# Weighted sums with the values as weights, two heads on the array's column halves, and the narrow projections of sparse attention packed into one tile

## What is computed

```python
# sparse attention: 8 heads, ONE key head and ONE value head of width 64, 4 index heads
xr, yr, q, k, v, iq, ik, iw = jnp.split(x @ w_in, ...)      # widths 512 512 512 64 64 256 64 4
dots = jnp.einsum("bthd,bsd->bths", iqb, ik)
isc = jnp.einsum("bths,bth->bts", jax.nn.relu(dots), iwb)   # then the best 128 of the causal keys
probs = jax.nn.softmax(logits, axis=-1)                     # logits with a slope per head
return jnp.einsum("bthk,btkd->bthd", probs, vsel)
# latent attention: 16 heads, keys of width 96, values of width 64, causal
probs = jax.nn.softmax(logits, axis=-1)
return jnp.einsum("bhts,bshd->bthd", probs, v)
```

## Time and profile before

| | |
|---|---|
| median of 3 runs | 2769.94 us (2769.45 to 2771.9) |
| the profiled execution | 2770.24 us, its span 2768.4 us |
| granted clock of TensorE, mean | 0.991 |
| PE busy | 2692.2 us, 97% of the span, 13514 records |
| DVE busy | 1228.7 us, 44% |
| ACT busy | 934.1 us, 34% |
| POOL busy | 921.5 us, 33% |
| sparse attention, first score to last turn-out | 1535.6 to 1602.6 us |
| latent attention, same | 2142.6 to 2295.0 us |

### The profile page before, as it was taken

How to read it: one execution, slowest core, us unless ns; L and a number is a source line. 1 busy time by engine, 2 the same in 40 slices (tenths; PEclk the granted TensorE clock), 3 DMA queues, 4 the chain that set the end, 5 groups by cost and what they waited for, 6 DMA issues and landing times.

```text
span 2768.4 us, 34791 instructions
## 1 busy us (share of the span) xinstructions
PE 2692.2 (97%) x13514; PEld 2214.7 (80%) x13514; DVE 1228.7 (44%) x1981; ACT 934.1 (34%) x1304; POOL 921.5 (33%) x221
## 2 busy tenths in 40 slices
PE   8999999999999999999999999999998999999998
PEld 7898787887788877888877788888876778888886
DVE  6566543353522234101269743704543564370453
ACT  3353422223433343222254534212234543421222
POOL 2321243444223213444432123444432112344441
PEclk9999999999999999999999999999999999999999
DMA  7531343543222212232221022222221112222221
GB/s 307 185 135 62 120 152 144 190 170 103 87 69 69 74 56 76 80 116 92 78 98 61 31 69 92 91 100 97 92 84 50 43 47 69 92 91 99 98 91 61
DMA packets 44170, 271.37 MB, mean 98 GB/s; under 512 B 5087, under 2 KB 8695, under 8 KB 15896
## 3 DMA queue, kind: packets, MB, share of 16 engines
q1 hardware_dynamic: 40032, 266.23, 27.4%
q10 hardware_dynamic: 4024, 3.54, 0.6%
HBM read 267.62 MB, written 2.13 MB: 97 GB/s over the span
## 4 chain that ended last, share of the span: by engine, by line
PE 69%; issue 22%; POOL 5%; DVE 3%; ACT 1%; POOLq 0%; DVEq 0%; ACTq 0%
PE lin L711 20%; PE lin L713 19%; PE lin L712 19%; POOL wlo L676 5%; PE lin L1243 2%; PE bank L1263 2%; PE bank L1255 1%; PE lin L853 1%; PE bank L1548 0%; PE bank L870 0%; PE bank L1419 0%; DVE tmp L3015 0%; PE bank L1399 0%; PE bank L1230 0%; ACT whi L1720 0%
## 5 line engine op out<-in xcount | busy, mean ns | idle before, releaser
L676 POOL TENSOR_TENSOR wlo<-raw,whi 128x2048 fp32r<-128x2048 f32 (+3 forms) x213 | 921.0, 4324 | 1809.7 <-ACT whi L1720 1809.7
L711 PE MATMUL lin<-hhi,whi 128*128 128x512 f32 x1976 | 782.6, 396 | 10.9 <-DVE hlo L2492 2.5
L713 PE MATMUL lin<-hhi,wlo 128*128 128x512 f32 x1976 | 770.7, 390 | 0.0
L712 PE MATMUL lin<-hlo,whi 128*128 128x512 f32 x1976 | 770.2, 390 | 0.0
L1720 ACT ACTIVATE whi<-raw 128x2048 fp32r<-128x2048 f32 (+3 forms) x213 | 384.3, 1804 | 949.8 <-PE lin L713 886.0
L711 PEld LDWEIGHTS lin<-hhi,whi 128*128 128x128 f32 x1976 | 371.6, 188 | 99.7 <-issue 11.8
L711 PE MATMUL lin<-ghi,whi 128*128 128x512 f32 x1120 | 438.8, 392 | 4.4 <-POOL wlo L676 2.4
L713 PE MATMUL lin<-ghi,wlo 128*128 128x512 f32 x1120 | 436.7, 390 | 0.0
L712 PE MATMUL lin<-glo,whi 128*128 128x512 f32 x1120 | 436.4, 390 | 0.0
L713 PEld LDWEIGHTS lin<-hhi,wlo 128*128 128x128 f32 x1976 | 371.3, 188 | 79.0
L712 PEld LDWEIGHTS lin<-hlo,whi 128*128 128x128 f32 x1976 | 371.7, 188 | 75.2 <-issue 1.2
(11 more groups left out here) (464 smaller groups left out, 2812.1 us busy)
## 6 DMA issues: line engine op xcount, KB each, us to landing
raw<-in_w SPq DMA_DIRECT2D x171, 1024.0 KB, 4.9
adw_a<-in_ada SPq DMA_DIRECT2D x30, 1024.0 KB, 5.0
adw_b<-in_ada SPq DMA_DIRECT2D x18, 1024.0 KB, 6.2
raw<-in_w SPq DMA_DIRECT2D x20, 768.0 KB, 4.4
raw<-in_w SPq DMA_DIRECT2D x16, 640.0 KB, 3.8
raw<-in_w SPq DMA_DIRECT2D x6, 512.0 KB, 3.5
x<-in_x SPq DMA_DIRECT2D x1, 2048.0 KB, 17.0
out<-x SPq DMA_DIRECT2D x8, 256.0 KB, 2.0
```

What stands on the lines that cost most here:

```text
L676: nc.gpsimd.tensor_tensor(wlo[:, slot, 0:size], raw[:, slot, 0:size], whi[:, slot, 0:size].bitcast(F32), ALU.subtract).then_inc(s.wlo_ok, 1)
L711: pe.matmul(dst, lh, rh, start=first, stop=False)
L712: pe.matmul(dst, lh, rl, start=False, stop=False)
L713: return pe.matmul(dst, ll, rh, start=False, stop=last)
```

## The change

The unit of 128 columns goes from the plan. Its 68 columns (v, iw, padding) now lie in the second unit, with ik and k once each; ACT copies ik and k to both halves of the partitions. The v and iw tile comes out with features on the partitions, is evicted to `m[:, 6]` and turned by four transposes (`turn_narrow`, placed in the first q tile). The index scores move from chunks 0 to 5 of the first q tile to its chunks 4 to 7 and the second tile's chunks 0 and 1. `early` becomes (1, 2, 4). `log_decay_scale` and the two activations before it move to the end of the dilated mixer.

In both attentions the weighted sum takes the values as weights (64 columns) and streams the turned exponentials (128 columns), for two steps (heads) at a time: one head to partitions 0 to 63, the other to 64 to 127 of one bank, product by product in turn (`weighted`). It runs at odd i for steps i-5 and i-4. Features are then on the partitions, and the turn-out, its transposes and its scaling go. The exponentials are scaled before they are turned: DVE takes the reciprocal of each row sum one step behind, and ACT scales the exponentials in place. The transposes run three steps behind the scores instead of two. There are three buffers of exponentials instead of two, four of turned blocks instead of two, and the outputs use B6 and B7 in turn.

```diff
-    plan += [("hy_in", DC, 256)] * 2 + [("hy_in", DC, 128)] + [("hy_in", DC, 256)] * 6
+    plan += [("hy_in", DC, 256)] * 8
...
-        sc5 = sb("sc5", [P, 2, T], F32, sc1 + 7168)
-        pt5 = [sb(f"pt5{i}", [P, 4, P], F32, sc1 + 11264 + 2048 * i) for i in range(2)]
+        sc5 = [sb(f"sc5{i}", [P, T], F32, sc1 + 7168 + 2048 * i) for i in range(2)] + [sq[:, 0, :]]
+        pt5 = [sb(f"pt5{i}", [P, 4, P], F32, (sc1 + 11264, sc1 + 13312, h_at, h_at + 2048)[i]) for i in range(4)]
...
-        sc7 = sb("sc7", [P, 2, T], F32, sc1 + 4096)
-        pt7 = [sb(f"pt7{i}", [P, 4, P], F32, sc1 + 8192 + 2048 * i) for i in range(2)]
-        os7 = sb("os7", [P, 256], F32, sc1 + 12288)
+        sc7 = [sb(f"sc7{i}", [P, T], F32, sc1 + 4096 + 2048 * i) for i in range(2)] + [sq[:, 0, :]]
+        pt7 = [sb(f"pt7{i}", [P, 4, P], F32, sc1 + 8192 + 2048 * i) for i in range(4)]
...
+            def attention(steps, banks, S, PT, before, between):
...
-                def turn_out(q):
...
-                for i in range(len(steps) + 4):
+                def weighted(p, q, u):
+
+                    bank, at = (B6, B7)[turns[0] % 2], slice(p.h // 2 * P, p.h // 2 * P + P)
+                    if p.first and turns[0] >= 2:
+                        pe.wait_ge(s.lo_ok, low + lows[turns[0] - 1])
+                        if chunks[turns[0] - 1]:
+                            pe.wait_ge(s.y_ok, done + chunks[turns[0] - 1])
+                    for b in range(q.j + 1):
+                        pe.matmul(bank[0:64, at], p.pick[b], PT[(u - 1) % 4][:, b, :], start=(b == 0), stop=(b == q.j))
+                        mm = pe.matmul(bank[64:P, at], q.pick[b], PT[u % 4][:, b, :], start=(b == 0), stop=(b == q.j))
+                    mm.then_inc(s.pv_mm, 1)
+                    if q.last:
+                        turns[0] += 1
+                        count = q.out.stop - q.out.start
+                        lows.append(lows[-1] + (1 if q.j < TT - 1 else 0))
+                        chunks.append(chunks[-1] + (count if q.j == TT - 1 else 0))
+
+                for i in range(len(steps) + 5):
...
-                    if i >= 4 and steps[i - 4].last:
-                        turn_out(steps[i - 4])
-                    if 2 <= i < len(steps) + 2:
-                        t, q = i - 2, steps[i - 2]
-                        pe.wait_ge(s.pr_ok, read + t + 1)
+                    if 3 <= i < len(steps) + 3:
+                        t, q = i - 3, steps[i - 3]
+                        pe.wait_ge(s.sp_ok, scaled + t + 1)
                         if t >= 2:
                             pe.wait_ge(s.pt_d, copied + t - 1)
                         for b in range(q.j + 1):
-                            mm = pe.transpose((B4, B5)[t % 2][:, b * P:(b + 1) * P], S[:, t % 2, b * P:(b + 1) * P], ident)
+                            mm = pe.transpose((B4, B5)[t % 2][:, b * P:(b + 1) * P], S[t % 3][:, b * P:(b + 1) * P], ident)
                         mm.then_inc(s.tr_mm, 1)
-                    if 3 <= i < len(steps) + 3:
-                        u, q = i - 3, steps[i - 3]
+                    if i >= 4 and i % 2:
+                        u = i - 4
                         pe.wait_ge(s.pt_d, copied + u + 1)
-                        if q.first and turns[0]:
-                            pe.wait_ge(s.o_ok, scaled + turns[0])
-                        for b in range(q.j + 1):
-                            mm = pe.matmul(B6[:, q.col:q.col + 64], PT[u % 2][:, b, :], q.pick[b],
-                                           start=(b == 0), stop=(b == q.j))
-                        mm.then_inc(s.pv_mm, 1)
+                        weighted(steps[u - 1], steps[u], u)
                     between(i)
                 n.up(s.pr_ok, len(steps))
                 n.up(s.pt_d, len(steps))
...
-                lin_pair(hin, s.h_ok)
-                pe.wait_ge(s.wlo_ok, n.up(s.wlo_ok))
-                tok_unit(st.u % 2, st.tile, DC, 128, 0, 128, hin)
-                st.u, st.tile = st.u + 1, st.tile + 4
+                evicted = n.at(s.ev_a) + 4
+                lin_pair(hin, s.h_ok, (1, 2, 4))
+
+                def turn_narrow():
+
+                    pe.wait_ge(s.ev_a, evicted + 3)
+                    for t in range(TT):
+                        tk = slice(t * P, (t + 1) * P)
+                        mm = pe.transpose(LB[(st.tile - 1) % 4][:, tk], m[:, 6, tk], ident)
+                    mm.then_inc(s.mm, 1)
...
+                        if j == t == 0:
+                            bank_free()
+                            st.tile += 1
...
+                                turn_narrow()
                             at = c * 256 + t * P
...
+                            if j == 0 and 0 <= k < (TT - 1) * IDX_H:
+                                if k == 0:
+                                    pe.wait_ge(s.ev_a, evicted + 4)
                                 index_scores(k)
-                    st.u, st.tile = st.u + 1, st.tile + 2
+                                index_scores(k + 1)
+                        st.tile += 1
+                    st.u += 1
...
+                            act.wait_ge(s.tr_mm, turned + i - 2)
                         top = mmax if q.scale == 1.0 else scaled_max
-                        act.activation(S[:, i % 2, 0:q.w], banks[i % len(banks)][:, 0:q.w], ACT.Exp,
-                                       bias=top[:, i % 4:i % 4 + 1], scale=q.scale, accum_out=rsum[:, col:col + 1]).then_inc(s.pr_ok, 1)
-                    if i >= 4 and steps[i - 4].last:
-                        q = steps[i - 4]
-                        out += 1
-                        act.wait_ge(s.ot_mm, out)
-                        act.activation(ghi[:, q.out, q.rows],
-                                       B7[:, 0:(q.out.stop - q.out.start) * P].rearrange("p (k t) -> p k t", t=P), ACT.Copy)\
-                            .then_inc(s.yt_ok, 1)
+                        act.activation(S[i % 3][:, 0:q.w], banks[i % len(banks)][:, 0:q.w], ACT.Exp,
+                                       bias=top[:, i % 4:i % 4 + 1], scale=q.scale, accum_out=rsum[:, i % 16:i % 16 + 1])\
+                            .then_inc(s.pr_ok, 1)
+                    if 1 <= i <= len(steps):
+                        t, q = i - 1, steps[i - 1]
+                        act.wait_ge(s.ri_ok, inverted + t + 1)
+                        act.activation(S[t % 3][:, 0:q.w], S[t % 3][:, 0:q.w], ACT.Identity, scale=rsum[:, t % 16:t % 16 + 1])\
+                            .then_inc(s.sp_ok, 1)
+                    if i >= 5 and i - 5 < len(steps) and steps[i - 5].last:
+                        q = steps[i - 5]
+                        act.wait_ge(s.pv_mm, weighted + (i - 4) // 2)
+                        act.activation(ghi[:, q.out, q.rows], (B6, B7)[turns % 2][:, 0:(q.out.stop - q.out.start) * P]
+                                       .rearrange("p (k t) -> p k t", t=P), ACT.Copy).then_inc(s.yt_ok, 1)
+                        turns += 1
                     between(i)
...
-                act.activation(qk[:, 2, :], LB[tile[0] % 4][:, :], ACT.Copy).then_inc(s.ev_a, 1)
+                packed, narrow = LB[tile[0] % 4], LB[(tile[0] + 1) % 4]
...
-                split_next()
-                act.activation(qk[0:64, 3, :], LB[(tile[0] + 1) % 4][0:64, :], ACT.Copy).then_inc(s.av, 1)
-                act.activation(kpad[64:P, :], LB[(tile[0] + 1) % 4][64:P, :], ACT.Copy).then_inc(s.ev_a, 1)
-                n.up(s.av)
+                act.activation(m[:, 6, :], narrow[:, :], ACT.Copy).then_inc(s.ev_a, 1)
+                act.activation(qk[0:64, 2, :], packed[0:64, :], ACT.Copy).then_inc(s.av, 1)
+                act.activation(qk[64:P, 2, :], packed[0:64, :], ACT.Copy).then_inc(s.av, 1)
+                act.activation(qk[0:64, 3, :], packed[64:P, :], ACT.Copy).then_inc(s.av, 1)
+                act.activation(kpad[64:P, :], packed[64:P, :], ACT.Copy).then_inc(s.ev_a, 1)
+                n.up(s.av, 3)
                 n.up(s.ev_a, 2)
                 tile[0] += 2
-                read(1, 4, ACT.Copy, lambda k: vi[:, k, :], P)
+                split_next()
...
+                def narrow_out():
+
+                    act.wait_ge(s.mm, n.up(s.mm))
+                    act.activation(vi[:, :, :].rearrange("p t n -> p (t n)"), LB[tile[0] % 4][:, :], ACT.Copy).then_inc(s.ev_a, 1)
+                    n.up(s.ev_a)
+                    tile[0] += 1
...
+                narrow_out()
...
+                    if k == 3:
+                        q_out(0)
...
-                    if 2 <= i < len(steps) + 2:
-                        t, q = i - 2, steps[i - 2]
+                    if 1 <= i <= len(steps):
+                        col = rsum[:, (i - 1) % 16:(i - 1) % 16 + 1]
+                        v.wait_ge(s.pr_ok, summed + i)
+                        v.reciprocal(col, col).then_inc(s.ri_ok, 1)
...
+                        if t >= 4:
+                            v.wait_ge(s.pv_mm, weighted + t // 2 - 1)
+                        v.tensor_copy(PT[t % 4][:, 0:q.j + 1, :],
...
```

(23 more changed lines are left out.)

100 lines of the change are left out of this document (39 added, 61 removed).

## The result

The changed kernel takes 2745.77 us (median, 2745.33 to 2747.08), the one before 2769.69 beside it: a ratio of 0.9911 (95% interval 0.9899 to 0.9922). Run again later, it took 2748.30 beside 2769.34. The forecast was 2746, and each of its three terms has its sign right. The first is nearly right in size, the other two are off by 2.9 us upwards and 2.75 us downwards, and the sum holds because these two cancel, which is luck.

What follows compares the result with a forecast made beforehand. PE was taken to bound the kernel, except where DVE sets the pace in sparse attention. Narrow projection 9.2, sparse attention 2.5 and latent attention 12.7 sum to 24.4 us off 2770.24, said as 2746 us, range 2736 to 2761.

Steps and rivals of the forecast that it cites:

- Narrow projection: Stretch where only PE works: its 96 products go, less transposes and waits, -9.2 us, ends -7.5 and -10.2.
- Rival (f): Something in the earlier weights or scores takes the narrow gain back, with a poor forecast: no change; chance 0.02.
- Price of a pair: Weighted sums on PE: two products on the two column halves cost 0.215 us together, 0.42 without overlap.
- rival (c): Weighted sums: the two column halves do not run together, a pair costs 0.42 us; 2764 us, chance 0.08.
- Rival (b): Weighted sums: weight loads do not hide behind the other half's stream, a pair costs 0.32 us; 2755.5 us, chance 0.06.
- Trip: PE's round trip into column strips and back, one per pair of steps, costs 0.30 us, ends 0 and 0.42.
- DVE and ACT at nothing: Both attentions: added reciprocals (about 0.1 us) and scalings (0.3 to 0.6 us) are hidden by slack and cost nothing.
- Sparse attention: DVE sets the pace for 20 of 32 steps, so mainly the last query block gains: -2.5 us, ends +2 and -6.
- Latent attention: PE is spared 16.3 us, of which 3.6 are not gained: -12.7 us, ends -6 and -19.
- rotation stretches: Latent attention, second query block of three head groups: DVE rotates the next queries, some 1.2 us each not gained.
- Rival (d): DVE and ACT set the pace in both attentions, only the narrow projection counts: 2761 us, chance 0.10.
- Rival (e): Sparse attention: with less PE work the clock falls to 0.50 and stays there, slower at 2781 us; chance 0.04.

Runs made afterwards that it cites:

- e_serial: Changed kernel, but in each pair all products of the first head come before all of the second, on the same column halves; 2754.23 us.
- e_trip: Changed kernel with one unused full-array transpose behind the first pair of products in 36 of 48 visits to the column halves; 2759.19 us.
- e_noscale: Changed kernel with ACT's scaling of the exponentials cut to their first column, so the output is not divided by the row sums; 2743.42 us.
- e_recip2: Changed kernel with a second reciprocal of the same column, into another column, before each reciprocal on DVE; 2748.29 us.
- e_best: Changed kernel with ACT's key copies at steps 2, 4, 7, 12 and DVE's query rotation at steps 3, 4, 6, 7, 8, 9; 2740.05 us.
- e_narrow: Kernel before with only the narrow projection packed, index scores and log decay's scale moved, nothing of the attention change; 2760.31 us.
- e_rot: Changed kernel with DVE's rotation of the next queries at steps 3, 8, 9, 10, 12, 13 of each sixteen instead of 3 to 8; 2754.41 us.
- e_keys: Changed kernel with ACT's four copies of rotated keys moved from steps 12 to 15 of latent attention to 2, 4, 7, 12; 2742.65 us.

## Why the prediction was right, point by point

- **Narrow projection**, 9.2 against 8.8: right; the first q tile starts at 1429.55, where the narrow products began before. Rival (f) did not occur, but it was nearer than its 0.02. The step let DVE's choice of the best keys "move along". It ended at 1513.4 instead of 1516.5 us, 2.1 us earlier counted from the mixer's first product and not 9, and DVE's idle time ahead of the first maximum of the sparse attention fell from 11.96 us to 2.88. Not even these 2.88 us are room, as the chain shows. DVE, POOL, ACT and PE of the changed kernel, and last ACT of the kernel before:

```profile
1514.02 6.90 DVE L3108 SCALAR_TENSOR_TENSOR wl<-wl,lr 128x512 f32<-128x512 f32 x4
1514.56 4.61 POOL L674 TENSOR_TENSOR wlo<-raw,whi 128x2048 fp32r<-128x2048 f32 x1 [26.93 <-ACT whi L1726]
1519.75 1.84 ACT L2305 ACTIVATE wl<-wl 128x512 f32<-128x512 f32 x3 [2.84 <-DVE wl L3108]
1523.49 1.90 ACT L1726 ACTIVATE whi<-raw 128x2048 fp32r<-128x2048 f32 x1
1525.93 0.38 PE L1243 MATMUL lin<-qk 128*128 128x128 f32 x1 [2.52 <-ACT m L1746]
...
1533.17 1.91 ACT L1720 ACTIVATE whi<-raw 128x2048 fp32r<-128x2048 f32 x1 [2.97 <-PE lin L713]
```

  DVE's operation behind the best keys is held by POOL, ACT waits for it, and ACT's split of the next weights starts 0.08 us after PE's last product (1523.41). Before, ACT had waited 2.97 us for that product. PE's first score waits for the eviction behind the split, 2.5 us in both kernels. So DVE and ACT have just caught up with PE here, and more taken off PE between the index scores and this point would not have shown. Not foreseen either: 1.9 us in the sparse attention, 1.4 of them by the clock under the dummy products.
- **Price of a pair**, 0.215 us: right, measured 0.218, where four records on one half alone take 0.436. What stood for rival (c), that PE takes records in order, is not quite so: it starts a record of the other half before up to three earlier ones. Rival (c) itself, 0.42 a pair, is out by the 0.218. Rival (b) is out: 64 columns of weights are loaded for each record (on either half a load of 0.14 us for every 0.109), and no record waits for one. The Trainium skill, TensorE: Matmul & The Clock Gate, Part 3, "What overlaps and what doesn't", has products in strict order of start; `e_serial` shows them out of order across the column halves.
- **Trip**, 0.30 us: right, 0.30 in the changed kernel and in `e_trip`.
- **DVE and ACT at nothing** (step 5): roughly right for sparse attention, wrong for latent. The scaling is 0.39, 0.50, 0.605 and 0.71 us for one to four key blocks, more than the 0.62 at most that was taken. Its cost is at least 0.4 + 2.2 us (`e_noscale`, which leaves 0.28 of each). The step counted ACT's sum, 100 of 133 us (103 of 142 in the trace), and not its queue: four copies that PE waits for at a fixed place stand behind four exponentials and now four scalings.
- **Sparse attention**, 2.5 against 5.4 (the step's own terms, 3.4 - 1.2 + 1.5 - 1, give 2.7): 1.9 came with the narrow change. Of the other 3.5, 2.37 lie in the last block, where 2.5 were forecast, and 1.15 in the first three, for which the step had nothing, since DVE sets the pace. It did, but a reciprocal costs DVE 0.07 and not 0.1 us, and three scalings of 0.7 with the waits on them went; that these make up the 1.15 us is argued, not shown. `e_recip2` shows that DVE's order counts there: 1.1 us for 32 x 0.07 = 2.2.
- **Latent attention**, 12.7 against 9.95: the failing term is "what counts". In the last group, where nothing lies beside, 16.3 / 4 = 4.1 us were to be had and 3.29 came, because PE now waits 0.37, 0.44 and 0.78 us there for copies and turns. In the first group it was 1.26, because of the key copies: a wait of 3.15 us instead of 1.21. With the low clock behind it, which costs 1.6 us in the second group, that is 3.5 us which the change lost at this border, more than the 2.75 by which the term was too large. The rotation stretches, with 1.2 us each as loss, were a real loss, by DVE's queue; their size was not measured by itself (`e_best` gets 1.9 us of it back in three groups). The mean of 1.45 us was read as the length of an operation. It is six of 0.68 and two held ones of 3.21 and 4.31.

Rival (d) is out as a whole: PE's waits for copies in latent attention are 3.6 us, below the 5 that were named. Rival (e) occurred in small: a stretch at 0.50 in both attentions, at no great price in sparse.

What stays open: why the clock falls later at the start of the sparse attention in `e_narrow` than before, and stays low for 5.8 us in `e_recip2` and some 4 in the changed kernel after the same wait; and how much of the gain in latent attention came by the shorter holds of DVE by POOL.

## What to carry to other kernels

Two small products on the two column halves cost as one when their records alternate, and each visit to the halves costs 0.3 us; but take visits away only where something else covers the exponentials. When work is added to an engine with room in its sum, look at what stands behind it in its queue at the places where the bounding engine waits for a last item, here four copies that could be made three to ten steps earlier. An average length of an operation can hide two kinds, plain and held ones: look at them one by one. Compare kernels by stretches between fixed first starts: here they repeated within 0.1 us, where the medians of the same kernel were 2.5 apart.

## What the runs showed of the hardware

- PE starts records of one column half ahead of up to three earlier ones of the other; records on the same half stay 0.109 us apart (`e_serial`).
- Leaving the column halves for one full-array record and entering them again cost 0.30 us (`e_trip`).
- A DVE addition from SBUF to SBUF waits until POOL's running subtraction has ended, 4.89 instead of 0.68 us (`e_rot`), and ends 0.54 to 0.56 us behind it, here with 32 partitions.
- After 3.15 us of waiting PE ran at 1.2 GHz for some 4 us in the changed kernel and 5.8 in `e_recip2`; where the wait was gone (`e_keys`) it did not.
